# Feed-forward up projections: 17 instead of 9 of 22 block pairs a layer by seven half products, with all forms in one five-slot buffer

## The reference

```
x = x + mixer_i(rms_norm(x))        # HGRN2, differential attention, RWKV-7, HGRN2
x = x + swiglu(rms_norm(x))
def swiglu(x, w_in, w_out):
    gate, up = split(x @ w_in, 2)   # w_in 1024 x 5632
    return (silu(gate) * up) @ w_out  # w_out 2816 x 1024
```

## Time and profile before

| what | value |
|---|---|
| median of three runs | 3167.41 us |
| lowest and highest | 3164.34 and 3167.78 us |
| time of the profiled execution | 3168.23 us |
| its span (first to last instruction) | 3166.7 us |
| mean granted TensorE clock | 0.985 |
| busy: TensorE matmuls | 3052.4 us (96%) |
| busy: VectorE | 2070.9 us (65%) |
| busy: ScalarE | 1230.9 us (39%) |

### The profile page before, as it was taken

One profiled execution on the slowest core, in us unless ns is written; L12 is line 12 of the kernel. 1 busy time (PEld: TensorE's weight loads), 2 busy tenths in 40 slices (PEclk: granted clock), 3 DMA queues, 4 the chain that ended last, 5 costly groups with the idle time before them and its releaser, 6 DMA issues.

```text
span 3166.7 us, 79404 instructions
## 1 busy us (share of the span) xinstructions
PE 3052.4 (96%) x32948; PEld 2869.7 (91%) x32948; DVE 2070.9 (65%) x3550; ACT 1230.9 (39%) x2089; POOL 131.3 (4%) x247
## 2 busy tenths in 40 slices
PE   8999999999999999997999998999999999999998
PEld 7998899999887999997997777999999889899997
DVE  6767774666666674666547886774665767775574
ACT  4223432333555432332336665442333323443231
POOL 0000000001332000000000000000000000000000
PEclk9999999999999999998999999999999999999999
DMA  3322222233444222222220001222222222222222
GB/s 131 97 92 76 82 93 93 80 108 99 135 130 114 81 89 91 91 98 73 69 75 12 21 25 28 81 93 88 92 97 83 88 88 85 86 80 97 78 106 74
DMA packets 104601, 269.08 MB, mean 85 GB/s; under 512 B 12802, under 2 KB 45954, under 8 KB 104146
## 3 DMA queue, kind: packets, MB, share of 16 engines
q1 hardware_dynamic: 91346, 228.54, 22.2%
q0 software_dynamic: 13056, 37.64, 3.5%
HBM read 247.61 MB, written 18.52 MB: 84 GB/s over the span
## 4 chain that ended last, share of the span: by engine, by line
PE 82%; DVE 10%; ACT 4%; DVEq 3%; issue 2%; DMA 0%; ACTq 0%; SPq 0%
PE ps L689 39%; PE ps L765 12%; PE ps L698 5%; PE ps L701 3%; PE ps L702 3%; PE ps L700 3%; PE ps L1225 3%; PE ps L699 3%; PE ps L1203 2%; PE ps L825 1%; DVE cell L2698 1%; ACT arena L1699 1%; DVE arena_r L2253 1%; PE ps L1235 1%; PE ps L1078 1%
## 5 line engine op out<-in xcount | busy, mean ns | idle before, releaser
L689 PE MATMUL ps<-arena_r 128*128 128x272 f32 x6816 | 952.4, 295 | 40.4 <-DVE arena_r L2246 14.8
L689 PEld LDWEIGHTS ps<-arena_r 128*128 128x128 f32 x6816 | 884.4, 191 | 85.5 <-issue 56.2
L689 PE MATMUL ps<-hb_r,arena_r 128*128 128x272 f32 x4992 | 643.7, 290 | 16.2 <-DVE arena_r L2278 15.9
L689 PEld LDWEIGHTS ps<-hb_r,arena_r 128*128 128x128 f32 x4992 | 637.2, 190 | 19.1 <-DVE arena_r L2278 9.4
L1647 ACT ACTIVATE arena_r<-ring 128x1024 fp32r<-128x1024 f32 (+1 forms) x168 | 198.0, 1179 | 450.9 <-PE ps L702 345.3
L698 PE MATMUL ps<-arena_r 128*128 128x480 f32 x704 | 269.6, 383 | 0.0
L2278 DVE TENSOR_TENSOR arena_r<-ring,arena_r 128x1024 fp32r<-128x1024 f32 (+1 forms) x168 | 231.1, 1375 | 35.1 <-ACT arena_r L1647 35.1
L2307 DVE TENSOR_TENSOR x<-x,ps 128x544 f32<-128x544 f32 x64 | 46.2, 722 | 290.8 <-PE ps L702 290.8
L765 PE MATMUL ps<-arena_r 128*128 128x272 f32 x1728 | 235.6, 289 | 0.0
L765 PEld LDWEIGHTS ps<-arena_r 128*128 128x128 f32 x1728 | 224.7, 188 | 0.0
L701 PE MATMUL ps<-arena_r 128*128 128x304 f32 x704 | 213.6, 303 | 0.0
(11 more groups left out here) (452 smaller groups left out, 4358.5 us busy)
## 6 DMA issues: line engine op xcount, KB each, us to landing
ring<-in_w_up SPq DMA_DIRECT2D x176, 512.0 KB, 3.5
ring<-in_w_mix SPq DMA_DIRECT2D x112, 512.0 KB, 3.5
ring<-in_w_down SPq DMA_DIRECT2D x64, 704.0 KB, 4.1
arena<-in_hg_s POOLq DMA_DIRECT2D x16, 512.0 KB, 3.8
out_hg_so<-arena POOLq DMA_DIRECT2D x16, 512.0 KB, 2.9
ring<-in_w_hgout SPq DMA_DIRECT2D x16, 512.0 KB, 3.5
arena<-in_cache_k SPq DMA_DIRECT2D x128, 64.0 KB, 1.9
arena<-in_cache_v POOLq DMA_DIRECT2D x128, 64.0 KB, 2.2
```

The lines of the kernel that those rows point to most:

```text
L689: mm = pe.matmul(PS[:, 2 * a + hf, 0:HALF], part[:, ws], rhs[:, o:o + HALF], start=start and n == 0, stop=stop and n == 2)
```

## The change

- Which pairs are sevens: `UP` gives a letter for each pair of a half. Half 0: plain 0, 1 and 10, sevens 2 to 9. Half 1: plain 0 and 10, sevens 1 to 9. That is 17 of 22 a layer, 68 in all.
- The forms (512 columns of weights each; a seven has 7, a plain pair behind the first has 4) go through five slots of high and low parts. DVE works on the low parts three forms ahead and on the sums five forms ahead (`ahead`), ACT makes the high parts four or more ahead.
- Pair p uses PSUM banks 4(p mod 2) to 4(p mod 2)+3. In a seven, the first product goes to bank `by`; ACT copies it into bank `bx`, onto which the sixth product is accumulated; `by` goes on through four more products, with copies to SBUF (`ff_u2`, `ff_u3`) between. All products open with a start flag but the one onto the copy.
- `ff_lin` is no longer multiplied by `rstd`: the linear factor stays in PSUM, and `gated` reads it there. `added` multiplies the down product by `rstd` instead, in five instructions for two (two for the last down product of a layer, which is made of six matmuls a block in two banks).
- At the begin ACT makes the first two forms of pair 1 ahead of the high parts of the turned tokens; DVE's turned tokens, forms and factor are in a new order.
- SP refills a weight slot as soon as DVE has made the last low part from it, not when TensorE is done with it.
- The hardware loops of the feed forward are written out.

```diff
+        ff_slots = 5
+        def ff_form(high, k):
+            o = 2 * KC * NT + (0 if high else 2 * SLOT) + k * HD2
+            return arena_r[:, o:o + HD2]
...
+        UP = ("PPSSSSSSSSP", "PSSSSSSSSSP")
...
+                skips = -(self.count - 4) % ff_slots
+                self.slot = [(j + min(j // 8, skips)) % ff_slots for j in range(self.count - 4)] + [0, 1, 3, 4]
...
@@ TensorE
+                        by, bx, bz = (4 * (p % 2) + n for n in range(3))
+                        form_product(0, by, plain_parts(0, 0), True, True)
+                        form_product(1, bz, turned_parts(0), True, True)
+                        pe.wait_ge(S("ff_cp"), nth_copy(layer, s, p, 0))
+                        form_product(2, by, turned_parts(1), False, True)
+                        pe.wait_ge(S("ff_cp"), nth_copy(layer, s, p, 1))
+                        form_product(3, bz, plain_parts(HC, HALF), False, True)
+                        pe.wait_ge(S("ff_cp"), nth_copy(layer, s, p, 2))
+                        form_product(4, by, turned_parts(2), False, True)
+                        form_product(5, bx, plain_parts(HC, 0), False, True)
+                        pe.wait_ge(S("ff_cp"), nth_copy(layer, s, p, 3))
+                        form_product(6, by, turned_parts(3), False, True)
...
@@ ScalarE, begin
+                        form_high(0)
+                        form_high(1)
+                        if not s:
+                            turned_high(0)
+                            form_high(2)
+                            root(norm_name(layer, "f"), 3)
+                            turned_high(1)
+                            form_high(3)
+                            for f in (2, 3):
                                 turned_high(f)
+                            silu(0)
...
@@ ScalarE, a seven
+                        if F.kinds[p - 1] == "S":
+                            silu(p - 1)
+                        form_high(j + 4)
+                        copied(0, PS[:, bank + 1, 0:HALF], 0)
+                        form_high(j + 5)
+                        gated_high(p - 1)
+                        copied(1, ff_z5, 2)
+                        form_high(j + 6)
+                        copied(2, ff_u2, 0)
+                        form_high(j + 7)
+                        form_high(j + 8)
+                        copied(4, ff_u3, 0)
+                        form_high(j + 9)
+                        form_high(j + 10)
...
@@ VectorE
+            def added(x, a, two_banks):
+                tail = ff_lin2[:, 0:TA]
                 dve.drain()
+                if two_banks:
+                    dve.tensor_tensor(halves(ff_gate), acc(a), halves(rstd[:, :]), ALU.mult)
+                    dve.drain()
+                    return dve.tensor_tensor(x, x, ff_gate, ALU.add)
+                dve.tensor_tensor(ff_gate, main(a), rstd[:, :], ALU.mult)
+                dve.tensor_tensor(tail, side(a), rstd[:, 0:TA], ALU.mult)
+                dve.drain()
+                dve.tensor_tensor(ff_gate[:, 0:TA], ff_gate[:, 0:TA], tail, ALU.add)
+                dve.drain()
+                return dve.tensor_tensor(x, x, ff_gate, ALU.add)
...
+                    def ahead(j):
+                        form_low(j + 3)
+                        form_sum(j + 5)
...
+                    def first_pair():
+                        if not s:
+                            turned_raw(0)
+                            turned_raw(1)
+                            form_low(0)
+                            form_low(1)
+                            turned_raw(2)
+                            turned_raw(3)
+                            form_low(2)
+                            factor(norm_name(layer, "f"))
+                            gate_evict(0, 0)
+                            form_low(3)
...
@@ VectorE, a seven
+                        gated(p - 1)
+                        ahead(j)
+                        ahead(j + 1)
+                        gated_low(p - 1)
+                        ahead(j + 2)
+                        ahead(j + 3)
+                        ahead(j + 4)
+                        sem, count = formed(layer, s, j + 3)
+                        dve.wait_ge(S("ff_cp"), nth_copy(layer, s, p, 2))
                         dve.drain()
+                        dve.wait_ge(S(sem), count)
+                        dve.tensor_tensor(ff_gate[:, HALF:NT], ff_u2, PS[:, bank + 2, 0:HALF], ALU.add)
                         dve.drain()
+                        dve.tensor_tensor(ff_gate[:, HALF:NT], ff_gate[:, HALF:NT], r2, ALU.mult)
+                        ahead(j + 5)
+                        dve.wait_ge(S("ff_cp"), nth_copy(layer, s, p, 3))
+                        dve.tensor_tensor(ff_lin2, ff_u3, ff_z5, ALU.add)
+                        sem, count = formed(layer, s, j + 5)
+                        dve.wait_ge(S(sem), count)
+                        dve.tensor_tensor(ff_gate[:, 0:HALF], PS[:, bank + 1, 0:HALF], r1, ALU.mult).then_inc(S("ff_g"), 1)
+                        ahead(j + 6)
```

More of the change, by code:

```diff
@@ new lines, in build, with upto_s, step_unit, step_form @@
+        forms = [Forms(kinds) for kinds in UP]
+        for f in forms:
+            assert f.kinds[0] == "P" and f.kinds[FU - 1] == "P" and len(f.kinds) == FU
+        assert UP[0][1] == "P"
+        def upto_s(layer, s, per):
+            return sum(per(t) for _ in range(layer) for t in range(2)) + sum(per(t) for t in range(s))
+        def step_unit(layer, s, n):
+            return upto_s(layer, s, lambda t: 2 + forms[t].count + KC) + n + 1
+        def step_form(layer, s, j):
+            return step_unit(layer, s, 1) + j + 1
@@ L719, in feed_forward @@
                     unit0, block0 = 2 * HU * layer + HU * s, FC * layer + FU * s
[L721 to L726, removed]
+                    def first_pair():
+                        pe.wait_ge(S("ff_glu"), block0 + (CREDITS["ff_glu"] if s else 1))
                         for g in range(2):
[L729 to L740 removed]
@@ L755, in turned_parts, with form_product @@
                             return [[ff_turned(f, part)[:, c * HALF:(c + 1) * HALF] for c in range(HC)] for part in range(2)]
-                        def form_product(bank, form, parts, step, start):
-                            pe.wait_ge(S("ff_wl"), pair_step(layer, s, i, 1, begin) + step)
-                            buf, w0 = ff_form[form]
+                        def form_product(k, bank, parts, start, stop):
+                            if p == 2 and not s and k in (1, 2, 4, 6):
+                                pe.wait_ge(S("ff_tl"), 8 * layer + 4 + {1: 1, 2: 2, 4: 3, 6: 4}[k])
+                            j = forms[s].first[p] + k
+                            pe.wait_ge(S("ff_wl"), step_form(layer, s, j))
+                            high, low = (ff_form(part, forms[s].slot[j]) for part in (True, False))
@@ L775, in seven @@
[L775 to L789, removed]
-                    pe.wait_ge(S("ff_glu"), block0 + FU - 1 + CREDITS["ff_glu"])
[L793 to L797, removed]
+                                ws = slice(c * P, (c + 1) * P)
@@ L2445, in feed_forward, with down_low @@
+                        ahead(j + 6)
+                    def down_low(m):
+                        ff_rest(layer, step_down(layer, s, m), HU * s + 2 * FU + m, SLOT)
+                    first_pair()
+                    for p in range(1, FU):
+                        (seven if F.kinds[p] == "S" else plain_pair)(p)
+                    gated(FU - 1)
+                    down_low(1)
+                    gated_low(FU - 1)
                     n0 = HU * s + 2 * FU
```

482 lines of the change are left out of this document (280 added, 202 removed).

## The result

The changed kernel took 3138.39 us (median of four runs, 3135.32 to 3142.08), the kernel before 3166.22 beside it. The ratio is 0.9913, with a 95% interval of 0.9896 to 0.993: 0.9% faster, where 1.4% (3122 us) was forecast. The time lies in the stated range (3106 to 3157), but above the part of the forecast itself (3108 to 3135) and in that of rival B, and the gain is 28 us of the 45 that I had added up. The profiled execution took 3139.27 us.

The account below looks back on a forecast made before the run. TensorE was taken to pace the steady part. The terms, -48.3 + 2.0 - 2.4 + 2.4 + 0.8 = -45.5 us, against the profiled 3168.23 gave 3122.7, forecast as 3122 us (1.4% faster), range 3106 to 3157.

Parts of the forecast that it names:

- the forecast itself: Whole kernel: TensorE and DVE about level in the sevens, 3108 to 3135 us; chance 0.60.
- rival B: Sevens: DVE clearly sets the pace, turn 10.75 to 11.15 us, by drains with waits or slower copy; 3132 to 3159; chance 0.22.
- signs of being wrong: In the profile after: sevens 11 us or more apart, or DVE idle in them while TensorE waits.
- saving: TensorE: 32 plain pairs of 12.08 us become sevens of 10.57, saving 48.3 us.
- begin of half 0: After the norm sums: 5.3 us lost again a layer; nothing gained in layers 0 and 3, 2.4 won in 1 and 2.
- begin of half 1: First seven: copy of product 0 ready 0.6 us late, 2.4 us lost over four layers, bounds 0 and 6.
- down products: Longer added (1.2 to about 2.2 us) hidden under 8.29 us; last one of layers 1 and 3 costs 0.8 together.
- DVE's own work: In a seven: 10.60 us a turn, 0.03 above TensorE's 10.57, so 2.0 us lost over 68; bounds 0 and 29.
- rival E: DVE records don't overlap where sevens follow one another: 11.36 us a turn, 3174 us, slower; chance 0.05.
- Do waits add to DVE's turn?: In sevens: DVE's 1.1 us wait before gated_low makes no period; turn is the larger of 10.57 and DVE's work.
- D: Sevens: DVE stands 1.1 us before gated_low every turn, ACT's forms and copies moving with DVE; turn 11.7, 3197 us; chance 0.07.
- Weights: SP's refill waits for a slot's last low part, weights wanted over 9 us later, landing takes 3.5: no cost.

Follow-up runs that it names:

- experiment 1: Changed kernel with one order on ACT altered: in a seven the high part of the gated tokens is made before form j+5; 3122.6 us.
- experiment 8: Changed kernel with the gated tokens' high part ahead of form j+5 and pair 2 of half 0 plain; 3105.3 us.
- experiment 9: Changed kernel without the multiplication of the second gate half by its token factor in the sevens (computation left out); 3121.79 us.
- experiment 2: Changed kernel with one order on DVE altered: gated_low of a seven comes after the next low part; 3121.72 us.
- experiment 3: Changed kernel with one more DVE instruction of 272 columns in each seven, right in front of gated_low; 3140.29 us.
- experiment 4: Changed kernel with one more DVE instruction of 272 columns in each seven, after ahead(j+4), outside the wait; 3157.17 us.
- experiment 5: Changed kernel with pair 2 of half 0 plain again, 16 sevens of 22 a layer; 3121.28 us.
- experiment 6: Changed kernel's code with the nine sevens a layer of the kernel before; 3148.9 us, ratio 0.9939.

## Why the prediction was right and wrong, point by point

- **The range.** That the time lies in it is partly luck. It lies above the forecast's own 3108 to 3135, and the range reached up to 3157 for the sake of rival B, whose causes (drains, a slower copy) the trace doesn't show. One of the signs of being wrong came true instead: DVE has idle time in the sevens while TensorE waits, "a wait that I took for hidden". The turn itself, 10.83, fell between the two signs that I had given (10.57 to 10.7, and 11 or more).
- **The account.** For the profiled executions the sum was -45.5 us and -29.0 was measured. By the traces the terms are: saving -48.3; the 56 sevens away from the begins +17.0 where I had +2.0; begin of half 0 -1.0 where I had -2.4; begin of half 1 +1.9 for +2.4; down products +0.8 for +0.8. Together -29.6.
- **TensorE, the saving of 48.3 us.** The work per pair was right: with waits away, a turn is 10.56 us in experiments 1, 8 and 9.
- **DVE's own work.** Forecast 10.60 us a turn, measured 10.53. The four bare drains cost 0.07 to 0.09; of the two with waits, one cost 0.10 and one 0.16. Records do overlap by 0.08 (463.19 against 462.84 + 0.43), so rival E is out. The Trainium skill (VectorE: DVE Perf Modes, "The DRAIN you can't avoid") says that the next operation doesn't start until the pipe is empty, and in the same paragraph that one which isn't held starts earlier. I had weighed only the first; the trace, with starts 0.08 us inside the record before, agrees with the second.
- **"Do waits add to DVE's turn?" This is the step that failed.** I wrote that "the turn is the larger of 10.57 and DVE's own work". It is the ring over ACT, 10.83. In front of the high part I counted the copy of product 0 and one form, "those two instructions wait for TensorE's product 0 only", and concluded that the wait "doesn't make a period". But form j+4 stands ahead of both in ACT's queue. It is a sum's form and waits for `form_sum(j+4)`, DVE's last instruction before `gated`. With this edge the way from there over ACT is 2.83 us against 2.53 of DVE's. It was there to be found: ACT's order and the sums for k from 1 to 4 are in the change as shown. The price: 15.0 us (17.0 for 2.0) of the 16.6 between the sum of 3122.7 and the profiled 3139.27.
- **Rivals.** B has the time right (3132 to 3159) by the wrong cause, drains or a slow copy. D has the cause: DVE waits in front of `gated_low` in every turn, because ACT's forms move along with DVE. I had priced it at 1.1 us, the wait of a turn that starts early, and given it 0.07; it was 0.30. Experiments 1 to 4 show the place. (D's remark that the gain is used up from a turn of 11.24 should say 11.27: 47.5 / 68 = 0.70 over 10.57, as the sum without DVE's term is -47.5.)
- **Begin of half 0.** Gap behind the norm sums gone: right. Two waits of 2.1 and 2.7 us in the first seven: by the starts in layer 0 there were three, 2.0, 1.6 and 1.5, together 5.1 for 4.8, and 0.67 for the 0.5 after them. The first is form 5, as laid out. The other two are ACT's copies and not form 7: the copy of product 0 stands behind form j+4, the edge that I missed in the ring, and the copy of product 1 behind the high part that waits for `gated`. So the total was near by another path. The forecast "nothing gained in layers 0 and 3" came out (0.5 and 0.6 us lost), and layers 1 and 2 won 1.0 each for 1.2. Experiments 5 and 6 show what this net hides: the new begin gains 24.1 us, and the seven behind it gives 23.1 back. The prediction tells both but adds up only the net, and so it didn't see that one letter of `UP` keeps the gain. Nor did it see the half clock behind the first wait, 1.5 us a layer.
- **Begin of half 1.** 0.5 us for a forecast 0.6.
- **Down products.** The longer `added` is hidden: layer 0's eight products of half 0 take 66.3 us before and after. (The section on the change says five instructions; it is four, 2.33 us for a forecast 2.2.) The 0.8 us for the last one came: layers 0 and 2 don't change, the first product of the mixer behind layer 1 starts 12.08 us after the norm sums for 11.70 before, and from the first down product of layer 3's half 1 to the end are 80.7 us for 80.3.
- **Weights.** No wait of DVE or TensorE for a transfer of up weights in the new order: right.

## What to carry to other kernels

When an engine that had slack gets close to the pace of the leading one, adding up its own instructions isn't enough: follow each wait of the helper engine back to the work of the engine itself, and add up every ring that closes without the leader. A wait of 0.30 us was paid there with 0.26 in a usual turn, and moving one instruction on either engine took it away; the wait of 0.24 in experiment 9, whose ring was shorter than the leader's turn, was free. And where a start-up phase overloads a helper, the cheaper algorithm for the leader can be the dearer one for a single pair: here one plain pair in place of a seven, in each of four layers, was worth 17 us.

## What the runs showed of the hardware that I had not expected

A copy by ACT from one PSUM bank to another took 0.38 us for 272 columns in all 68 sevens; I had allowed for up to 0.6. The copies into SBUF took 0.37 to 0.38 (product 1) or 0.40 us (products 2 and 4), so nothing here says that the target makes the difference. A wait of 0.26 us inside a run of like matmuls is not printed by the timeline: 24 matmuls over 3.44 instead of 3.19 us is all that shows, so the distance between starts has to be read. TensorE's granted clock fell to half in some of the gaps at a begin and not in others (in the changed kernel in layer 3 alone, in experiment 1 in layer 0, 0.50 from 396 to 400 us, too); what decides this no run here shows. Writing out the hardware loops cost nothing that shows: instruction loads grew from 2.54 to 3.41 MB by the page, and TensorE's products keep their 1.51 us.
